# Differential-attention sub-norms moved a step later, the rotated key a step sooner, and more identity turns at the start

## The reference

```
u = rmsnorm(h, g_mix);  z = u @ w_in              # latent parts, rotary key, differential q, k, v
q, k, v of 8 latent heads from c_q, c_kv           # k has the rotated key in 32 of its rows, shared by heads
o_mla = softmax(q k^T * scale) v
w = softmax(q0 k0^T * s + bias) - lam * softmax(q1 k1^T * s + bias)     # 4 differential heads
o = w @ v
o_diff = rmsnorm(o, g_sub, 1e-5) * (1 - lam_init)  # the sub-norm, per head over its 128 columns
h = h + concat(o_mla, o_diff) @ w_out
h = h + square(relu(rmsnorm(h, g_mlp) @ w_up)) @ w_down
```

## Time and profile before

| | |
|---|---|
| median of 3 runs | 1206.96 us (1206.27 to 1208.67) |
| profiled execution | 1210.87 us |
| its span | 1209.0 us, so 1.87 us lie around it |
| mean granted TensorE clock | 0.993 |
| busy: PE, DVE, ACT, POOL | 98%, 73%, 50%, 48% |
| chain that ended last, by engine | PE 93%, DVE 2%, POOL 2%, DMA 1% |

### The profile page before, as it was taken

One profiled execution on the slowest core, in us unless ns is written; L12 is line 12 of the kernel. 1 busy time (PEld: TensorE's weight loads), 2 busy tenths in 40 slices (PEclk: granted clock), 3 DMA queues, 4 the chain that ended last, 5 costly groups with the idle time before them and its releaser, 6 DMA issues.

```text
span 1209.0 us, 16359 instructions
## 1 busy us (share of the span) xinstructions
PE 1189.2 (98%) x5672; PEld 974.2 (81%) x5672; DVE 882.8 (73%) x1356; ACT 600.4 (50%) x986; POOL 582.3 (48%) x371
## 2 busy tenths in 40 slices
PE   8999999999999999999999999999999999999997
PEld 7887678888888888888887776888888888888886
DVE  4657867656779776889856677776658778767896
ACT  5345766743544344435423466666444544344443
POOL 1014554622865676565510145537047665766462
PEclk8999999999999999999999999999999999999999
DMA  5521110134234322431324201102342334223402
GB/s 160 157 70 62 45 24 30 53 87 147 76 92 139 106 90 87 137 105 36 105 58 121 70 27 44 36 18 88 86 159 89 87 105 140 88 81 111 140 13 92
DMA packets 128132, 104.56 MB, mean 86 GB/s; under 512 B 5514, under 2 KB 107956, under 8 KB 128052
## 3 DMA queue, kind: packets, MB, share of 16 engines
q1 hardware_dynamic: 127840, 103.50, 28.9%
q10 hardware_dynamic: 84, 0.02, 0.0%
q0 software_dynamic: 128, 0.00, 0.0%
HBM read 99.84 MB, written 2.10 MB: 84 GB/s over the span
## 4 chain that ended last, share of the span: by engine, by line
PE 93%; DVE 2%; POOL 2%; DMA 1%; ACT 1%; issue 1%; SPq 0%; POOLq 0%; DVEq 0%; ACTq 0%
PE bank L1520 82%; PE bank L1590 3%; PE bank L1618 3%; PE bank L1561 2%; DMA stage<-in_w_in 1%; POOL rs L621 1%; PE bank L1538 1%; DMA xin<-in_x 1%; DVE k_pack L1177 0%; PE bank L1698 0%; PE bank L1690 0%; PE bank L1547 0%; PE bank L1753 0%; DVE w_lo L1066 0%; POOL e_x L630 0%
## 5 line engine op out<-in xcount | busy, mean ns | idle before, releaser
L1520 PE MATMUL bank<-u_hi,w_hi 128*128 128x512 f32 x760 | 299.3, 394 | 0.3
L1520 PE MATMUL bank<-u_hi,w_lo 128*128 128x512 f32 x760 | 296.1, 390 | 0.0
L1520 PE MATMUL bank<-u_lo,w_hi 128*128 128x512 f32 x760 | 295.9, 389 | 0.0
L750 ACT ACTIVATE w_hi<-stage 128x1024 fp32r<-128x1024 f32 (+2 forms) x141 | 136.4, 977 | 225.8 <-DMA stage<-in_w_up 92.2
L1066 DVE TENSOR_TENSOR w_lo<-stage,w_hi 128x1024 fp32r<-128x1024 f32 (+2 forms) x116 | 136.6, 1187 | 57.6 <-ACT w_hi L750 57.2
L1520 PEld LDWEIGHTS bank<-u_hi,w_hi 128*128 128x128 f32 x760 | 142.8, 188 | 31.0 <-issue 2.5
L1520 PEld LDWEIGHTS bank<-u_hi,w_lo 128*128 128x128 f32 x760 | 142.7, 188 | 30.3
L1520 PEld LDWEIGHTS bank<-u_lo,w_hi 128*128 128x128 f32 x760 | 142.9, 188 | 28.3
L750 ACT ACTIVATE w_hi<-b 128x1024 fp32r<-128x1024 f32 x84 | 89.0, 1059 | 129.8 <-PE bank L1520 88.8
L1520 PE MATMUL bank<-w_hi,quad_hi 128*128 128x512 f32 x392 | 152.6, 389 | 0.0
L1520 PE MATMUL bank<-w_hi,quad_lo 128*128 128x512 f32 x392 | 152.5, 389 | 0.0
(11 more groups left out here) (237 smaller groups left out, 2293.6 us busy)
## 6 DMA issues: line engine op xcount, KB each, us to landing
stage<-in_w_up SPq DMA_DIRECT2D x64, 512.0 KB, 4.1
b<-in_w_down SPq DMA_DIRECT2D x56, 512.0 KB, 3.5
stage<-in_w_in SPq DMA_DIRECT2D x32, 512.0 KB, 3.9
stage<-in_w_out SPq DMA_DIRECT2D x16, 512.0 KB, 3.6
stage<-in_w_down SPq DMA_DIRECT2D x8, 512.0 KB, 3.4
xin<-in_x SPq DMA_DIRECT2D x4, 512.0 KB, 7.1
stage<-in_w_ukv SPq DMA_DIRECT2D x4, 512.0 KB, 3.5
out<-yout SPq DMA_DIRECT2D x8, 256.0 KB, 2.4
```

The lines of the kernel that those rows point to most:

```text
L750: last = nc.scalar.activation(hi(w_hi, s)[:, :, d:d + n], st(r)[:, :, f:f + n], ACT.Copy)
L1520: mm = nc.tensor.matmul(acc, a, b, start=first and t == 0 and m == 0, stop=last and t == len(terms) - 1 and m == 2)
```

## The change

Of each sub-norm, the broadcast on PE goes from n = 9+4g, behind the scores, to n = 10+4g, behind the fillers and ahead of the scores; the power on POOL from step 8+4g to 9+4g, so behind the next `t1` or `normalise`; the scale on DVE from the end of n = 9+4g to n = 10+4g, behind the two `ttr` (or the row maximum). The rotated key's two parts go to n = 11 on ACT and n = 12 on DVE. At the start, 12 more turns of the identity follow the gains' turn, and 5 more stand between the first and the second pair of turns of x.

```diff
--- before.py
+++ after.py
@@ -709,7 +709,7 @@
                     else:
                         normalise(l, n - 1 - DSTEPS)
                     g, r = divmod(n - 8, TT)
-                    if r == 0 and 0 <= g < DIFF_HEADS:
+                    if r == 1 and 0 <= g < DIFF_HEADS:
                         power(l, MISC_AT[f"sub{g}_c"], 3 + g, rs)
                     for use in ended(n - 2):
                         if use[0] == "q":
@@ -931,7 +931,7 @@
                     g, r = divmod(n - 7, TT)
                     if r == 0 and 0 <= g < DIFF_HEADS + MLA_HEADS:
                         pv_out(l, g)
-                    if n == DSTEPS - 4:
+                    if n == DSTEPS - 5:
                         act.wait_ge(kr_ready, val(kr_ready, l, 2))
                         act.wait_ge(sc_done, val(sc_done, l, 2 * (DSTEPS - TT)))
                         nc.scalar.activation(k_pack[NOPE:P, 0, 0, :], krf[NOPE:P, :], ACT.Copy).then_inc(krb_hi_made, 1)
@@ -1344,14 +1344,19 @@
                         inverse_sum(l, n - 1 - DSTEPS)
                         if n < STEPS:
                             row_max(l, n - DSTEPS)
+                    g, r = divmod(n - 8, TT)
+                    if r == 2 and 0 <= g < DIFF_HEADS:
+                        dve.wait_ge(misc_done, val(misc_done, l, MISC_AT[f"sub{g}_b"] + 1))
+                        nc.vector.scalar_tensor_tensor(out=tmp_s[:, 0, :], in0=tmp_s[:, 0, :], scalar=cols(gsl, 0, l),
+                                                       in1=MISC_BANK[:, :], op0=ALU.mult, op1=ALU.mult
+                                                       ).then_inc(misc_free, 1)
                     if HEAD_USES[-1] in ended(n - 3):
                         split(l, BLOCK_AT[(HEAD_USES[-1], 0)] + RING)
                     if "kp1" in ended(n - 2):
                         gen_low(l, "kp1")
-                    g, r = divmod(n - 8, TT)
                     if r == 0 and DIFF_HEADS <= g < DIFF_HEADS + MLA_HEADS - 1:
                         pv_out(l, g)
-                    if n == DSTEPS - 3:
+                    if n == DSTEPS - 4:
                         dve.wait_ge(krb_hi_made, val(krb_hi_made, l, 1))
                         nc.vector.tensor_tensor(k_pack[NOPE:P, 0, 1, :], krf[NOPE:P, :],
                                                 k_pack[NOPE:P, 0, 0, :].bitcast(F32), ALU.subtract
@@ -1373,12 +1378,6 @@
                         dve.wait_ge(misc_done, val(misc_done, l, MISC_AT[f"sub{g}_c"] + 1))
                         nc.vector.scalar_tensor_tensor(out=rc[:, :], in0=MISC_BANK[:, 0:TT], scalar=1.0 / (2 * DIFF_D),
                                                        in1=eps0[:, g % 2 * TT:(g % 2 + 1) * TT], op0=ALU.mult, op1=ALU.add
-                                                       ).then_inc(misc_free, 1)
-                    if r == 1 and 0 <= g < DIFF_HEADS:
-
-                        dve.wait_ge(misc_done, val(misc_done, l, MISC_AT[f"sub{g}_b"] + 1))
-                        nc.vector.scalar_tensor_tensor(out=tmp_s[:, 0, :], in0=tmp_s[:, 0, :], scalar=cols(gsl, 0, l),
-                                                       in1=MISC_BANK[:, :], op0=ALU.mult, op1=ALU.mult
                                                        ).then_inc(misc_free, 1)
                     if r == 1 and g >= DIFF_HEADS and (g - DIFF_HEADS) % 2 == 1 and g < DIFF_HEADS + MLA_HEADS - 1:
                         hd = g - DIFF_HEADS
@@ -1675,10 +1674,15 @@
 
 
             pe.wait_ge(consts_made, 4)
-            for i in range(16):
-                nc.tensor.transpose(bank[7][:, 0:P], ident[:, :], ident[:, :])
+            def keep_busy(count):
+
+                for i in range(count):
+                    nc.tensor.transpose(bank[7][:, 0:P], ident[:, :], ident[:, :])
+
+            keep_busy(16)
             pe.wait_ge(gm_in, 16)
             nc.tensor.transpose(bank[1][:, 0:G_MLP], g_rows[0:G_MLP, :], ident[0:G_MLP, 0:G_MLP]).then_inc(gt_done, 1)
+            keep_busy(12)
 
             def first_turn(j):
 
@@ -1697,7 +1701,10 @@
                     for m, w in enumerate(wtile(SLOT[0], k)):
                         nc.tensor.matmul(bank[BANK["cq0"]][:, :], w, u_hi[:, k, :], start=(k == 0 and m == 0), stop=False)
 
-            for j in range(4):
+            for j in range(2):
+                first_turn(j)
+            keep_busy(5)
+            for j in range(2, 4):
                 first_turn(j)
             pe.wait_ge(gt_copied, 1)
             pe.wait_ge(gm_in, 16)
@@ -1805,12 +1812,12 @@
                             latent_sum(l, use)
                     if n >= STEPS - 1:
                         out_sum(l, OUTM_USES[n - STEPS + 1], range(0, 2))
+                    if r == 0 and 0 < g <= DIFF_HEADS:
+                        stat_b(l, MISC_AT[f"sub{g - 1}_b"], 2 + g)
                     if n + 1 < DSTEPS:
                         score_pair(l, n + 1)
                     if r == 2 and 0 <= g < DIFF_HEADS:
                         stat_c(l, MISC_AT[f"sub{g}_c"], tmp_s[:, 1, :])
-                    if r == 3 and 0 <= g < DIFF_HEADS:
-                        stat_b(l, MISC_AT[f"sub{g}_b"], 3 + g)
                     if r == 3 and g >= DIFF_HEADS:
                         half_values(l, g + 1, 0)
                     if r == 0 and g == DIFF_HEADS:
```

## The result

| | before | changed |
|---|---|---|
| median | 1208.53 us (1206.27 to 1208.9, 6 runs) | 1213.74 us (1211.54 to 1216.6, 6 runs) |
| profiled execution, span | 1210.87, 1209.0 us | 1215.95, 1214.1 us |
| mean granted clock of the profiled execution | 0.993 | 0.994 |

The ratio is 1.0047, 95% interval 1.0032 to 1.0061: slower by 5.7 us (3.9 to 7.4). The prediction was 1206.4 with a range to 1209.3, 0.6 us under the median it started from: the change came out on the other side.

A forecast was written before the change was run, and what follows sets the result against it. PE was taken as the bound, busy 1189.2 of 1209.0 us. Start 2.9 us gained less 2.3 lost in two layers made 0.6 under the median 1206.96: 1206.4 us, 8-in-10 range 1202.6 to 1209.3.

The forecast's parts named there:

- start: First 20 us: identity turns fill PE's gaps and hold the clock, second latent sum at 17.2, not 20.17; gain 2.9 us.
- key: Rotated key: VectorE's low part moves to where VectorE waits anyway, ScalarE's high part costs nothing; counted within head 1.
- head 3: Fourth head's sub-norm: broadcast moves to where PE had no gap, 0.4 plus a 1.0 wait; loss 1.4 us per layer.
- head 2: Third head's sub-norm: a 0.4 wait before turn(16) goes, an uncovered 1.0 comes; loss 0.65 us per layer.
- if it is down: Other case for the start: at the lower clock 12 turns take 2.6 us, first turn of x slips to 7.9.
- the 3.9 us between profile and median: Profiled execution above the median: read as two clock falls in the layers (3.4 us) that most timed runs lack.
- Head 0: First head's sub-norm: turn(8) starts 1.1 us earlier without the root, less broadcast and wait; net gain 0.6 per layer.
- head 1: Second head's sub-norm: turn(12) starts 1.8 us sooner with head 0's 0.6, less broadcast and waits; adds 0.3 per layer.
- The clock in the layers: Idle before turn(12) cut to about 0.6, so 140:160 stays up; 3.4 us against the profiled execution, none against the median.
- Rival 3: New waits at head 1 or head 3 bring the clock down in the layers: 3.4 us more, 1209.8; chance 0.06.
- rival 2: Extra turns don't save the start; layers' 2.3 us loss remains, up to 1.1 added: 1209.3 to 1210.4; chance 0.12.

The follow-up runs named there:

- experiment 1: The kernel before with only the 12 and 5 further identity turns at the start: 1207.56 us, ratio 0.9993.
- 6: The kernel before with the 17 further identity turns and the rotated key a step sooner, no sub-norm moved: 1207.62 us, ratio 0.9999.
- 3: The changed kernel with the sub-norms of heads 2 and 3 put back; heads 0 and 1, key and start as changed: 1207.66 us, ratio 1.0003.
- experiment 12: Heads 0 and 1 and key moved, heads 2 and 3 not, 6 and 5 identity turns, v0's low part first on VectorE in step 9: 1206.76 us, ratio 0.9986.
- experiment 2: The change without the identity turns and with the key in its old place, so the sub-norms alone moved: 1216.96 us, ratio 1.0083.
- 10: Kernel before with start and key changed, and VectorE's low parts of the key and of kp1 behind the turned block's: 1208.99 us, ratio 1.0011.
- experiment 7: The change with 12 identity turns into MISC_BANK while PE waits for the low part at head 3: 1213.39 us, ratio 1.0046.
- 8: Kernel before with the start's further turns, and 8 and 12 identity turns ahead of the turns of blocks 8 and 12: 1208.48 us, ratio 1.0010.
- experiment 5: Start and key as in the change, only head 3's sub-norm moved: 1209.95 us, ratio 1.0027.
- experiment 9: The changed kernel with the broadcasts of heads 2 and 3 ahead of the filler of their step: 1210.00 us, ratio 1.0021.

## Why the prediction was wrong, by its steps

Ratios of one experiment to another give each term for both layers: start -0.8 us (experiment 1), key +0.7 (6 against 1), heads 0 and 1 +0.5 (3 against 6), head 3 +3.4, head 2 +1.6, in sum +5.4 of the 5.7 measured. Each is known to 1.3 to 2.1 us, so of the single terms only head 3's is clear of zero; heads 2 and 3 together, +5.0, are too.

Two steps failed, and they make 5.1 of the 6.3 us between the forecast (-0.6) and the result (+5.7). Heads 0 and 1 with the key were to give 1.8 us and cost 1.2, because VectorE's low parts and POOL's difference hold each other up. The start was to give 2.9 us of the median and gave 0.8, because it was priced on a profiled execution that is an extreme one. Heads 2 and 3 were to cost 4.1 and cost 5.0.

By another route, an estimate: PE's waits in the layers are 11.9 us in the change's profile and 7.4 before, 4.5 more. The mean clocks (0.9960 in its six runs, 0.9972 in the 92 of before, 0.9966 to 0.9978 by chip) add about 1.4 (0.7 to 2.2), and the start is in them, for all of experiment 1's gain can be clock (0.9977 for 0.9968 is 1.1 us). That makes 5.9 of waits and clock for 5.7 measured.

- **The start, 2.9 us.** The mechanism held: 2.39 us in the profiles, clock 1.00, the second latent sum at 17.78. The size was off by the 12 turns, which ran at the lower clock (the sum took them at 0.12 us; "if it is down, 12 turns are 2.6 us" stood in the text as the other case). But the step that failed is the next one: the gain was worked out against the profiled execution and then taken whole from the median. I had read the 3.9 us between profile and median as falls that the median lacks, gave them all to the layers, and kept the start's low stretch for every run. But 52 of the 92 executions of before are at 0.998 or 0.999, too high for the whole of that stretch: the usual run lacks it as well. Gain of the median 0.8.
- **Head 0, +0.6 per layer; head 1, +0.3.** Turn(8) did start 1.3 us sooner (127.52 to 131.21, less 2.39), as "1.1 earlier" said, and all of it was lost again by head 0's value product (134.09 for 134.07, experiment 12). What failed is that VectorE's low parts were taken over with their old durations. In the kernel before the query's low part goes first and POOL's difference waits, which is why it took 1.78 us (129.37); the prediction read the 1.78 as its length. In the change the order is turned round (VectorE before, then POOL in the change):

```profile
129.34 0.68 DVE L1164 TENSOR_TENSOR dq_lo<-tmp_y,dq_hi 128x512 fp32r<-128x512 f32 x1
```

```profile
126.18 1.29 POOL L630 TENSOR_TENSOR e_x<-e_x 128x512 f32<-128x512 f32 x1
```

The low part now takes 1.07 for 0.68 ahead of v0's (kp0 waits 0.50), and the key's 1.38 for 0.98 (turn(11) waits 0.34, the scores 0.73, 0.62 before). Turn(12) starts at 144.97, with 2.39 at 147.36: 0.5 us sooner than before and not 1.8. Experiments 2 and 10 show the cause, and 12 takes v0's part of it away and gets head 0's gain; the key's part was not taken away in any run. The text said "the rotated key's low part leaves its place for one where VectorE waits anyway", which was so, and it ran beside POOL there.
- **Head 2, -0.65.** Right: its product starts at 164.42, with 2.39 for the start 166.81, so 1.68 late against 165.13, of which head 1's product already was 1.07 late; 0.61 are head 2's. By the runs it is 1.6 us for both layers, not clear of the intervals.
- **Head 3, -1.4.** Right in size: from the turn's start to the product are 5.55 us (174.95 to 180.50), 2.53 before; in experiment 7, where the clock stays up there, they are 4.03 (174.01 to 178.04), so 1.5 without the clock. The runs give 3.4 for both layers, 2.8 of it forecast.
- **The clock in the layers.** Wrong. "The change cuts the second to about 0.6, so the clock should stay up" came true in the wait (0.61) and not in the clock, which fell in the first layer at that very turn, and at head 3 in both. Rival 3 named this with a chance of 0.06 and 3.4 us. The mean clocks put it lower, at about 1.4 of the 5.7 us, since runs of before have falls too. Experiments 7 and 8 do not settle the price: the first only moved the low stretch, the second kept PE longer than the gap lasted. In experiment 2 the clock was 4.6 us of the 10.
- **The rivals.** What came was rival 2's layers and small start, with heads 0 and 1 giving nothing: start -0.8, layers +6.2 in place of +2.3. Each rival took one step as failed and kept the others, so none reached 1213; and none priced POOL and VectorE on each other.

Still open is what decides whether the clock falls after a gap: the same wait (1.64 and 1.65) went with a fall in one kernel and without in another, and in experiment 5 both happened in one execution.

## What to carry to other kernels

Before an operation is brought forward on one engine, look at what runs on the other engines in the time it moves into, and whether those two can run together; here an earlier difference on GpSimd stopped VectorE's SBUF-only low parts, and at one of the two places it was cured by giving that time to an operation that reads PSUM. A bank that is handed on needs work between its filling and its next user: put the broadcast ahead of the filler, not behind it (experiment 9, 3.1 us less than the change). And compare the profiled execution with the spread of the timed runs first: a gain measured on stretches that only an extreme run has is not a gain of the median.

## What the runs showed of the hardware

- VectorE's low parts with two SBUF inputs and GpSimd's difference run one after the other. VectorE's 64x512 low part: 0.69 us alone, 1.38 and 1.54 behind a difference of 1.29, and 0.98 in the kernel before, beside GpSimd's scaling (145.40 to 146.17); the 128x512 one 0.68 and 1.07. GpSimd's difference, when it came second, 1.78 for 1.29; its root, second, 1.48 for 1.02. The root in first place held no low part up (0.68 us at 127.87 in experiment 12). Low parts that read a PSUM bank keep 0.67 to 0.69 us beside all of these.
- Turns of the identity alone bring the clock from its lower to its full level: the 12 turns at 5.52 still took 0.21 us each, and the eight turns of x at 7.85 took 0.13 each, and between 1.70 and 7.85 PE ran nothing but turns of the identity and the small one of the gains. By the Trainium skill's page "TensorE: Matmul & The Clock Gate" (Part 4) they would not; the traces disagree.
- The mean granted clock of one and the same kernel went from 0.993 to 0.999 over its 92 executions, and its span, in the mean of those at each, from 1209.0 to 1204.4 us with it: 0.4%, twice what most edits here were worth.
